# A recurrence solved on 64-token blocks, and value rows of a keyed expert layer summed earlier

## The reference, cut to what matters

```python
sa = einsum('bhij,bhj->bhi', state, -kk_t)
state = state * w_t + sa[..., None] * (kk_t * a_t) + v_t[..., None] * k_t
y_t = einsum('bhij,bhj->bhi', state, r_t)
```

```python
q = (xb @ w_q).reshape(t, 8, 2, 128)            # two sub-queries per head
s = einsum('thpd,hpkd->thpk', q, sub_keys)      # 128 keys on either side
idx, gate = best 16 of the 256 pairs, softmax   # idx in 0 .. 16383
h = gelu(einsum('thkd,td->thk', u_table[idx], xb))
out = einsum('thk,thkd->td', gate * h, v_table[idx])
x = layer_norm(x + out)                         # ALPHA is 2**0.25 on x
```

## Time and profile before

| | us |
|---|---|
| median of 3 runs | 2830.22 (2829.77 to 2835.93) |
| the profiled execution, its own time | 2829.56 |
| its span in the profile | 2827.6 |
| PE busy | 2508.5 (89%) |
| DVE busy | 1905.2 (67%) |
| ACT busy | 1044.7 (37%) |
| POOL busy | 673.2 (24%) |

### The profile page before, as it was taken

The page is one execution under the profiler, slowest core; times in us unless marked ns, Lnnn a source line. Parts: engine busy times, 40 slices in busy tenths (PEclk is TensorE's granted clock), DMA queues, the critical chain, the costliest instruction groups (busy, mean ns, idle before and its releaser), DMA issues. The chain is left out here.

```text
span 2827.6 us, 32278 instructions
## 1 busy us (share of the span) xinstructions
PE 2508.5 (89%) x11766; PEld 1876.8 (66%) x11766; DVE 1905.2 (67%) x3343; ACT 1044.7 (37%) x1886; POOL 673.2 (24%) x626
## 2 busy tenths in 40 slices
PE   3999839999986999867888988999999999999990
PEld 2875637888874866547886767888888874444440
DVE  5649447888874215675553648999589976666669
ACT  3238436877763236530002231111677740000000
POOL 0000011211200000200000003344466665444444
PEclk8999959999997989988898999999999999999995
DMA  7841146687662331220001238999899999999997
GB/s 271 276 174 73 52 188 247 267 322 297 266 251 79 93 82 45 64 67 12 1 1 68 67 90 260 318 333 331 308 409 409 406 387 410 409 409 409 409 409 299
DMA packets 271516, 655.21 MB, mean 232 GB/s; under 512 B 25472, under 2 KB 140416, under 8 KB 255872
## 3 DMA queue, kind: packets, MB, share of 16 engines
q1 hardware_dynamic: 189280, 376.28, 36.7%
q0 software_dynamic: 82080, 276.88, 25.5%
HBM read 662.50 MB, written 34.60 MB: 247 GB/s over the span
## 5 line engine op out<-in xcount | busy, mean ns | idle before, releaser
L2574 POOL DMA_INDIRECT sp_rows<-in_u_rows,sp_flat x184 | 221.5, 1204 | 726.5 <-DVE sp_flat L3009 524.0
L285 DVE TENSOR_TENSOR wide_low<-wide_raw,wide_high 128x2048 fp32r<-128x2048 f32 x138 | 312.5, 2291 | 63.5 <-ACT wide_high L278 61.5
L2742 PE MATMUL ps<-xT,raw 128*128 128x256 f32 x1536 | 342.5, 379 | 0.3 <-DMA raw<-in_u 0.3
L2772 PE MATMUL ps<-raw,tb_made 128*128 128x512 f32 x768 | 335.1, 592 | 0.8 <-DMA raw<-in_v 0.8
L2742 PEld LDWEIGHTS ps<-xT,raw 128*128 128x128 f32 x1536 | 287.9, 190 | 37.7 <-DMA raw<-in_u 0.7
L171 DVE TENSOR_TENSOR w_low<-raw,w_high 128x1024 fp32r<-128x1024 f32 x90 | 110.0, 1224 | 248.2 <-ACT w_high L162 247.8
L278 ACT CAST wide_high<-wide_raw 128x2048 fp32r<-128x2048 f32 x138 | 261.6, 1915 | 22.0 <-PE ps L335 15.9
L2772 PEld LDWEIGHTS ps<-raw,tb_made 128*128 128x128 f32 x768 | 145.8, 190 | 184.4 <-issue 182.7
L2583 DVE SCALAR_TENSOR_TENSOR sp_rows<-sp_rows,sp_x 128x1024 f32<-128x1024 f32 x184 | 223.0, 1221 | 22.6 <-DMA sp_rows<-in_u_rows,sp_flat 18.3
L2592 DVE SCALAR_TENSOR_TENSOR sp_x<-sp_rows,sp_coef,sp_x 128x1024 f32<-128x1024 f32 x118 | 150.6, 1287 | 72.3 <-DMA sp_rows<-in_v,sp_flat 71.8
L2909 ACT ACTIVATE pe_root<-pe_root 128x1 f32<-128x1 f32 x4 | 0.8, 203 | 501.5 <-issue 477.5
(11 more groups left out here) (516 smaller groups left out, 5400.6 us busy)
## 6 DMA issues: line engine op xcount, KB each, us to landing
wide_raw<-in_w_experts SPq DMA_DIRECT2D x96, 1024.0 KB
raw<-in_u SPq DMA_DIRECT2D x96, 512.0 KB
raw<-in_v SPq DMA_DIRECT2D x96, 512.0 KB
ada_raw<-in_ada_w SPq DMA_DIRECT2D x24, 1024.0 KB, 7.7
raw<-in_w_in SPq DMA_DIRECT2D x42, 512.0 KB, 3.8
raw<-in_peer_w_q SPq DMA_DIRECT2D x32, 512.0 KB
tb_ring<-in_u SPq DMA_DIRECT2D x32, 512.0 KB
tb_ring<-in_v SPq DMA_DIRECT2D x32, 512.0 KB
```

The source lines that it names most:

```text
L285: self.m.nc.vector.tensor_tensor(self.low_of[:, n % self.READY, :], self.raw[:, n % self.RAW, :], self.high_of[:, n % self.READY, :].bitca ...
L2574: self.m.nc.gpsimd.indirect_dma_start(out=self.rows(g), out_offset=None, in_=src, in_offset=bass.IndirectOffsetOnAxis(ap=self.flat[:, tile ...
L2742: last = nc.tensor.matmul(m.ps[:, HID + r % 2, 0:DT], u[:, c, :], m.xT[:, c, 0:DT], start=c == 0, stop=c == KT - 1)
L2772: last = nc.tensor.matmul(m.ps[:, Y + 2 * n + half, :], made[:, r, n * P:(n + 1) * P], v[:, half * T:(half + 1) * T], start=r == 0, stop=r ...
```

## The change

**Recurrence.** Every 128x128 matrix of a pair of chunks becomes two 64x64 blocks, one for each chunk c, on partitions 64c to 64c+63 and 64 columns wide. The zero quarters are neither stored nor computed. A matmul of 128 rows, 128 weight columns and 128 moving columns becomes two with 64, 64 and 64: c = 0 reads partitions 0 to 63 and writes 0 to 63, c = 1 reads and writes 64 to 127, both into the same PSUM bank. Products are no longer per head: two passes (fp) of 16 matmuls with 2x64 moving columns, over chunk c (output partitions) and head parity par (input partitions), then 16 `lower_products`. VectorE reads 512 columns at a time for A and 256 for N, Y, U and Ti. U's product now stands ahead of Ti's in a level, with a semaphore of its own for Ti (`ti_done`). The outputs split in two: what comes from the states (`outputs_from_states`) after Y of level 2, the rest after Y of level 3; the banks are two, one per chunk. Masks are made in a scratch tile and their diagonal quarters copied (`keep`).

```diff
@@ masks
+    masks.whole = sb("mask_whole", [P, P])
+    masks.part = sb("mask_part", [P, 2, CHUNK])
+    masks.low, masks.same = sb("mask_low", [P, CHUNK]), sb("mask_same", [P, CHUNK])
...
+    def keep(out, src=whole):
+        for c in range(2):
+            at = slice(c * CHUNK, (c + 1) * CHUNK)
+            last = nc.gpsimd.tensor_copy(out[at], src[at, at])
+        link(last)
@@ TensorE
+            def products(it, fp):
...
+                for k in range(2):
+                    f = 2 * fp + k
+                    for x, src in enumerate((w.b, w.k)):
+                        for c in range(2):
+                            for par in range(2):
+                                rows = rows_of(par)
+                                out = m.ps[chunk(c), P1_AT + 2 * fp + par, :].rearrange("p (y k x t) -> p y k x t", y=2, k=2, x=2)
+                                last = nc.tensor.matmul(out[:, :, k, x, :], src[rows, f, chunk_tokens(it, c)],
+                                                        KR[rows, it % 2, f, c, :, :], start=True, stop=True)
+                last.then_inc(p1, 1)
...
             def level_y(it, l):
                 for g in range(2):
                     pe.wait_ge(inv, it * INV + 2 * l + g + 1)
-                    for h in group(g):
-                        last = nc.tensor.matmul(m.ps[:, Y_AT + g, (h % H2) * P:(h % H2 + 1) * P], N[:, h, :],
-                                                U[:, it % 2, h, :], start=True, stop=True)
+                    for f in range(F):
+                        for c in range(2):
+                            last = nc.tensor.matmul(m.ps[chunk(c), Y_AT + g, cols(f)], N[chunk(c), g * F + f, :],
+                                                    U[chunk(c), it % 2, g * F + f, :], start=True, stop=True)
                     last.then_inc(y_done, 1)
...
+            def outputs_from_states(it):
+                pe.wait_ge(s_next, 2 * it + 3)
+                for f in range(F):
+                    for c in range(2):
+                        for par in range(2):
+                            rows = rows_of(par)
+                            last = nc.tensor.matmul(m.ps[rows, YO_AT + c, cols(f)], S[rows, (2 * it + c) % 3, f, :],
+                                                    KR[rows, it % 2, f, c, 1, :], start=f == 0, stop=False, skip_group_check=True)
+                last.then_inc(yo_begun, 1)
@@ TensorE's order
                 if new:
                     level_tu(it, 1)
+                    level_y(it, 2)
+                if old:
+                    outputs_from_states(it - 1)
+                if new:
+                    level_tu(it, 2)
+                    level_y(it, 3)
                 if old:
                     outputs(it - 1)
-                for l in range(2, LEVELS if new else 2):
-                    level_y(it, l)
+                for l in range(3, LEVELS if new else 3):
+                    if l >= 4:
+                        level_y(it, l)
                     level_tu(it, l)
```

```diff
-FIRST_QUAD = 57
+FIRST_QUAD = 53
+RING_FIRST = 28
-    early = 4 * [3] + first + choice + 2 * (4 * [3] + choice) + [6]
-    rows = [2 + r % 2 if r > FIRST_QUAD else 0 for r in range(KEYS)]
+    early = 4 * [3] + first + choice + 2 * (4 * [3] + choice) + [10]
+    rows = [0 if r <= FIRST_QUAD else 2 + r % 2 if r <= FIRST_QUAD + QUADS else 3 for r in range(KEYS)]
@@ GpSimd
             for g in range(2 * DOTS):
+                if g == DOTS + RING_FIRST:
+                    pool.wait_ge(residual, 1)
                 sparse.gather(pool, g)
@@ TensorE
             pe.wait_ge(lowered, QUADS)
+            add_x()
             for r in range(KEYS):
                 product(r)
-                if r == 2:
-                    add_x()
@@ VectorE, the u loop and after it
+                if r in SPARSE_GATE_ROWS:
+                    softmax(len(DENSE) + SPARSE_GATE_ROWS.index(r))
+                if dots_by(r - 3) == DOTS:
+                    sums(ROW_SUMS)
...
-            dve.wait_ge(residual, 1)
-            dve.wait_ge(placed_i, QUADS)
-            dve.wait_ge(gated, QUADS)
-            dve.sem_inc(sparse.spare_free, 1)
+            sums(DOTS)
-EXP_ROWS = (30, 47, 125, 126)
+EXP_ROWS = (26, 43, 100, 101)
+SPARSE_GATE_ROWS = (117, 118)
+ROW_SUMS = 3
-TURN_ROWS = (48, 54)
+TURN_ROWS = (44, 50)
```

More of the change, by code:

```diff
@@ new lines, in outputs @@
+            def outputs(it):
+                pe.wait_ge(yo_begun, it + 1)
+                for f in range(F):
+                    for x, src in enumerate((SA, Vt)):
+                        for c in range(2):
+                            for par in range(2):
+                                h = 2 * f + par
+                                left = SA[chunk(c), h, :] if x == 0 else Vt[chunk(c), it % 2, head_cols(h)]
+                                last = nc.tensor.matmul(m.ps[rows_of(par), YO_AT + c, cols(f)], left,
+                                                        A[chunk(c), 1 + it % 2, place(h), x, :], start=False, stop=x == 1,
+                                                        skip_group_check=True)
@@ L2148, in first_inverses @@
+                link(nc.vector.tensor_tensor(Ti[:], over(same[:], HEADS), Ti[:], ALU.subtract))
                 dve.wait_ge(inv, it * INV + 2)
@@ L2197, in _ @@
                     state_w(it - 1, 0)
[L2198 to L2199 removed]
+                if new:
+                    read_products(it, 0)
+                    read_products(it, 1)
+                    read_lower(it)
                 if old:
@@ L3045, in merge, with weigh, sums @@
                                         ).then_inc(merged, 1)
+            made_sums = [DOTS]
+            def weigh(s):
+                for batch in (s // BATCH, SLOTS_EACH // BATCH + s // BATCH):
+                    sparse.weigh(dve, batch)
+                dve.wait_ge(sparse.weighted, 2 * (s // BATCH + 1))
+            def sums(n):
+                for g in range(made_sums[0], min(made_sums[0] + n, 2 * DOTS)):
+                    tile, s = sparse.which(g)
+                    if tile == 0 and s % BATCH == 0:
+                        weigh(s)
+                    if g == DOTS:
+                        dve.wait_ge(sparse.started, len(SPARSE))
+                    sparse.add(dve, g)
+                    if g in NORM_AT:
+                        k = NORM_AT.index(g)
+                        if k == 0:
+                            dve.wait_ge(ln_loaded, 32)
+                        moments(k)
+                        normalise(k)
+                    made_sums[0] = g + 1
             for group in GROUPS:
```

269 lines of the change are left out of this document (129 added, 140 removed).

## The result

The changed kernel takes 2695.78 us (median of 4 runs, 2693.02 to 2700.44), the kernel before 2833.07 us in the same job (2829.77 to 2838.67). The ratio is 0.9515, 95% interval 0.9492 to 0.9538. The profiled execution took 2697.12 us with a span of 2695.0, so 132.4 us less than the one before; the forecast was 109, and the result lies 2 us under the range. Now and then an execution of any of these kernels takes some per cent longer at a lower clock (2946.78 us for one of the four of the first experiment); such executions are left out of every time here.

The account below looks back on a forecast made before the run. Bounds: the recurrence's chain of TensorE and VectorE in turns, then full DMA engines after a hole, with a tail of v-row adds. Recurrence 95 and experts 14 us off 2829.6 give 2720.6 us; own range 2698 to 2742, extended to 2768.

Parts of the forecast that it names:

- The price of a record: Recurrence: a 64-column record, chunks alternating, costs 0.035 us, between 0.0625 (one quarter at a time) and 0.031.
- Levels: Recurrence: a level with Ti falls from 6.41 to 3.57 us, 16 such levels gain 45.4 us.
- Products: Start of each recurrence tile: 9.4 us falls to 5.4, 16 us over four tiles.
- First inverses and first Y: Recurrence tiles: inverses gain 8 us; first Y to U falls from 3.4 us to 1.3 to 1.9.
- 4 us back: Recurrence: state parts lay partly in TensorE's gaps of a level, now smaller, so 4 us are lost.
- the two terms: Recurrence: last tile's outputs with the state products gain 4 us; values times masked products fall from 1.9 us to 1.1.
- Experts: Keyed experts: DMA hole closed, tile 0's norm no longer waits for a gather; gain 14 us, between 4 and 18.
- The margin of four: V loop: 229 v rows added when it ends, while the norm of tile 0 stands behind add 225.
- 1: Rival, recurrence: the two chunks' quarters do not overlap, since they write one bank; 2762 us, chance 0.12.
- 3: Rival, recurrence: slower, one quarter at a time at half clock; 2943 us, chance 0.03.
- Rival 2: Recurrence: nothing overlaps, or the clock is at half for most of it; 2797 us, chance 0.10.
- Rival 4: Recurrence: records narrower but the chain does not move, VectorE and delays set the level; 2815 us, chance 0.03.

Follow-up runs that it names:

- the first experiment: The kernel before with the changed kernel's masks and recurrence, keyed experts as they were; 2709.49 us median of 3 runs (same run as e1).
- e1: The kernel before with the changed kernel's masks and recurrence, keyed experts as they were; 2709.49 us, ratio 0.957.
- e2: The kernel before with the changed kernel's keyed experts, masks and recurrence as they were; 2817.18 us, ratio 0.9941.
- m3: Changed kernel, each lower product issued four times, alternating two quarters that share neither rows nor columns, then the other two; 2707.6 us, one run.
- m4: Changed kernel, each lower product issued four times, alternating two quarters that share their rows, then the other two; 2708.0 us, one run.
- e6: Changed kernel plus identity transposes into a free bank where TensorE idles (first inverses, waits of the last tile's chain); 2687.38 us, ratio 0.9492.
- e13: Changed kernel with parity outermost and chunk innermost in products and lower products, so neighbours alternate between two quarters only; 2695.41 us, ratio 0.9521.
- e11: The kernel before plus 32 identity transposes into a free bank while VectorE makes the first inverses; 2823.61 us, ratio 0.9971.
- e12: Changed kernel with the products of keys and state (state_w) in the old order, parity outermost; 2699.53 us, ratio 0.9532.
- e8: Changed kernel with no v rows added beside the last u rows (0 for 3 per row from row 122); 2702.34 us, ratio 0.9545.
- e5: Changed kernel with both pieces of the outputs back between level 1 and level 2; 2697.11 us, ratio 0.9526.
- e10: Changed kernel with the Ti and U products alternating per pair of heads, Ti first; 2695.95 us, ratio 0.9515.
- e3: Changed kernel with all matmuls of chunk 0 ahead of all of chunk 1 in each group of a level; 2703.82 us, ratio 0.9545.

## Why the prediction was right or wrong

**What bounds it** held: the recurrence is a chain, the experts are at the DMA limit, and the two don't meet (e1, e2).

**The price of a record** (0.035 us) was high by a fifth: 0.029 in a level. The step "the pair's rate and a little for starts" added that little for nothing. Two quarters in turns run at 0.029 between borders (m3, m4). **Levels:** by tile 1, four times 12.3 us gained, so 49.0 for 45.4. The inner levels last 3.08 for the 3.57 forecast; level 0 lasts 4.46, since the half clock falls on it (3.08 with the idle stretch filled, e6).

**Products, 16 forecast, 23.5 measured: wrong.** Tile 1 gained 5.0 us for the 4.0 forecast. The term "64 records at 0.053, in pairs" did not see that four quarters take turns: they ran at 0.027, and those 32 of 64 columns at 0.013. And pairs do not cost what that step says either: in runs of 16 they ran at 0.031, and e13 lost 0.4 to 0.5 us a tile, not 2.1. The other half of the miss comes from pricing the stretch in the first tile, where no state part stands in it; tiles 2 to 4 gained 1.2 us more each (14.0 to 7.9 us).

**First inverses and first Y:** the inverses gained 7.8 us for 8. From the first Y to the first product tile 1 gained 2.2 us for the 1.5 forecast, tiles 2 to 4 3.1 to 3.8.

**State parts, "4 us back": the step that failed most.** The forecast let them lose their cover in the gaps of a level; they took less time instead, 12.6 us of the miss. What tiles 2 to 4 have beyond tile 1 falls in two places. In levels 1 to 3, where the outputs stand, it went from 16.7 to 5.1 us: 11.6 gained, for the 13 of the outputs. In the products, the first Y and level 0, where most of the state parts stand, it went from 15.4 to 6.8 us: 8.6 gained, where the forecast lost 4. Of the 8.6 us the clock makes about 1.3 (with the idle stretch filled in both kernels, e11 and e6, 7.3 are left), and the new order of `state_w` about 1 (e12). The remaining 6 us were not tested, and their cause stays open.

**Half clock:** it cost 8.8 us after the first inverses before the change and 5.9 after it (e11, e6), and those 2.9 us are part of the gains above. **Last tile's chain, values in it:** 7.5 us, for the 4.8 of the two terms, since I halved only the outputs. The parts of it weren't tested one by one.

**Experts, 14 forecast, 14.6 measured: right, partly by luck.** The tail is 59.0 us from the norm as forecast. The u loop grew by 5.4 us at its start, just past the 5 that the forecast set as a sign of being wrong: it waited 6.3 us for its first rows, for 1.0 before, while the stage ahead of it ran 3.6 us shorter. That makes 1.8 us in sum, near the 2 that I had put there for another reason, the exponentials. And 225 adds were done when the v loop ended, not 229, and a stretch at 251 GB/s stayed, where the forecast's sign was no window under 380. The hole was closed only in part, and the 10 rows that came of it are just those that the norm needed. The margin of four that I counted wasn't there: e8 loses 6.6 us at once.

**Rivals.** 1 and 3 rested on the two chunks not overlapping because they write one bank. The levels' records (0.029 us, two row halves into one bank, disjoint partitions) refute it. By the Trainium skill, TensorEngine Tiling (Array Packing), section Restrictions and Gotchas, they could not have access at the same time; the trace does not bear that out for disjoint partitions. Rival 2's slow clock exists but is 9 us (e6), and its other half, that nothing overlaps, is refuted by the same records. Rival 4 is refuted by the period.

## What to carry to other kernels

When small matmuls fit a part of the array, price a record by how many parts take turns in the stream, one pace divided by one, two or four, and look for loops whose order reaches all four. When a forecast's terms are compared with a trace, cut the trace at the same events as the terms, or time seems to have no term when it only lies in another piece: the read of U comes 1.2 to 3.8 us behind the product that the levels' term began with. Price what is woven into a loop from the iterations that have it, as well as from the one that doesn't; here that was worth 11 us. Where TensorE idles for 3 us ahead of a dense stretch, harmless transposes into a free bank are worth a trial: e6, with a median of 2687.4 us, is the fastest kernel here. Its ratio to before, 0.9492, and the changed kernel's, 0.9515, have intervals that overlap; that it is faster than the changed kernel rests on the recurrence in the profiles, 128.4 us for 137.7 to 139.1, and on e5 and e10 in its own job, which differ little from the changed kernel and took 2697.1 and 2696.0 us.

## What was not expected of the hardware

- Two orders of records cross. In e3 a run of level_tu's second product starts in one quarter while the first product's last records are still starting in the other, as its timeline shows:

```profile
1292.36 0.27 PE L2015 MATMUL ps<-rc_Ti,rc_Y 64*64 64x64 f32 x1
1292.41 0.22 PE L2009 MATMUL ps<-rc_Y,rc_Ti 64*64 64x64 f32 x1
1292.47 0.22 PE L2015 MATMUL ps<-rc_Ti,rc_Y 64*64 64x64 f32 x1
1292.47 0.22 PE L2009 MATMUL ps<-rc_Y,rc_Ti 64*64 64x64 f32 x1
1292.53 0.22 PE L2015 MATMUL ps<-rc_Ti,rc_Y 64*64 64x64 f32 x1
1292.53 0.22 PE L2009 MATMUL ps<-rc_Y,rc_Ti 64*64 64x64 f32 x1
```

All of this group's L2009 records stand ahead of its L2015's in the stream, and three of the latter start before the last of the former. The Trainium skill, TensorE: Matmul & The Clock Gate, section Part 3: Packing small matmuls, says that matmuls start strictly in program order; here the records of different quarters do not.

- At half clock (granted clock 0.50) a record of a level takes 0.054 us for 0.029, a little less than twice (sixteen from 1289.44 to 1290.30).
- Filling an idle stretch of 3 us held the granted clock at 0.99 over the recurrence, for 0.89.
